# Two transformer blocks in one kernel: another order of work between the output projection and the first weight pairs

## The reference, cut to what matters

```python
x = x + jnp.einsum('bse,ed->bsd', y_mix, w_out[l])
h = rms_norm(x, norm2_g[l])            # x * rsqrt(mean(x*x) + eps) * g
u = causal_dwconv(jnp.einsum('bsd,df->bsf', h, w_up[l]), ffn_conv_w[l])
gate, up = jnp.split(u, 2, axis=-1)
x = x + jnp.einsum('bsf,fd->bsd', jax.nn.gelu(gate) * up, w_down[l])
```

## Time and profile before

| what | value |
|---|---|
| median of 3 runs | 1773.47 us (1772.86 to 1775.33) |
| the profiled execution | 1773.04 us |
| its span in the profile | 1771.3 us |
| mean granted clock of TensorE | 0.982 |
| TensorE busy | 1705.1 us (96%) |
| VectorE busy | 1179.0 us (67%) |
| ScalarE busy | 791.0 us (45%) |
| GpSimd busy | 538.3 us (30%) |

### The profile page before, as it was taken

The page is one execution under the profiler, slowest core; times in us unless marked ns, Lnnn a source line. Parts: engine busy times, 40 slices in busy tenths (PEclk is TensorE's granted clock), DMA queues, the critical chain, the costliest instruction groups (busy, mean ns, idle before and its releaser), DMA issues.

```text
span 1771.3 us, 20806 instructions
## 1 busy us (share of the span) xinstructions
PE 1705.1 (96%) x7516; PEld 1383.2 (78%) x7516; DVE 1179.0 (67%) x1406; ACT 791.0 (45%) x1022; POOL 538.3 (30%) x297
## 2 busy tenths in 40 slices
PE   6999999999859999999999999998999999999998
PEld 5888878888647888888888888887878877666786
DVE  6577671379888776676676789885636455666554
ACT  5566631245434444444444444553422155666531
POOL 4222122100055455455553000003433242444320
PEclk9999999999879999999999999998999999999999
DMA  7111112063302322322323965651322220110251
GB/s 252 48 47 36 47 48 72 24 220 114 119 11 85 95 73 81 95 71 83 91 75 107 342 217 186 224 160 42 119 72 71 84 71 24 36 48 25 89 220 71
DMA packets 159896, 176.96 MB, mean 100 GB/s; under 512 B 13390, under 2 KB 114516, under 8 KB 159828
## 3 DMA queue, kind: packets, MB, share of 16 engines
q1 hardware_dynamic: 157524, 167.67, 29.4%
q10 hardware_dynamic: 2304, 8.39, 1.3%
HBM read 140.38 MB, written 35.65 MB: 99 GB/s over the span
## 4 chain that ended last, share of the span: by engine, by line
PE 87%; DVE 7%; ACT 3%; issue 1%; POOL 1%; DMA 0%; DVEq 0%; ACTq 0%
PE ps L895 27%; PE ps L2282 25%; PE ps L2230 19%; PE ps L2481 5%; PE ps L2451 3%; PE ps L2466 2%; PE ps L2511 2%; PE ps L2454 2%; PE ps L2453 1%; DVE lat L1993 1%; DVE hop_lo_P L1802 1%; PE ps L2438 1%; DVE hop_mix_P L1796 1%; DVE square_dve L1580 0%; DVE scr L1737 0%
## 5 line engine op out<-in xcount | busy, mean ns | idle before, releaser
L919 POOL TENSOR_TENSOR w_lo<-w_raw,w_hi 128x1024 fp32r<-128x1024 f32 x52 | 136.0, 2617 | 622.5 <-ACT w_hi L1035 622.5
L2282 PE MATMUL ps<-hop_hi_P,wop_hi_P 128*128 128x512 f32 x672 | 266.9, 397 | 25.8 <-DVE hop_lo_P L1802 12.8
L2282 PE MATMUL ps<-hop_lo_P,wop_hi_P 128*128 128x512 f32 x672 | 265.8, 395 | 0.0
L2282 PE MATMUL ps<-hop_hi_P,wop_lo_P 128*128 128x512 f32 x672 | 265.3, 395 | 0.0
L895 PE MATMUL ps<-h_hi,w_hi 128*128 128x512 f32 x752 | 235.6, 395 | 13.3 <-DVE h_lo L1565 9.8
L895 PE MATMUL ps<-h_lo,w_hi 128*128 128x512 f32 x752 | 233.7, 392 | 0.0
L895 PE MATMUL ps<-h_hi,w_lo 128*128 128x512 f32 x752 | 233.4, 392 | 0.0
L925 POOL TENSOR_TENSOR wop_lo_P<-pair_raw,wop_hi_P 128x512 fp32r<-128x512 f32 x72 | 113.3, 1574 | 243.6 <-ACT wop_hi_P L1046 243.5
L895 PEld LDWEIGHTS ps<-h_hi,w_hi 128*128 128x128 f32 x752 | 142.0, 190 | 44.9 <-issue 15.9
L2282 PEld LDWEIGHTS ps<-hop_hi_P,wop_hi_P 128*128 128x128 f32 x672 | 128.7, 192 | 55.1 <-issue 13.6
L925 POOL TENSOR_TENSOR wop_lo_P<-pair_sum,wop_hi_P 128x512 fp32r<-128x512 f32 x96 | 132.0, 1376 | 125.4 <-ACT wop_hi_P L1046 125.4
(11 more groups left out here) (337 smaller groups left out, 3274.4 us busy)
## 6 DMA issues: line engine op xcount, KB each, us to landing
pair_raw<-in_w_up SPq DMA_DIRECT2D x48, 512.0 KB, 4.7
w_raw<-in_w_in SPq DMA_DIRECT2D x46, 512.0 KB, 3.9
dn_raw<-gu_park SPq DMA_DIRECT2D x84, 256.0 KB, 3.9
dn_raw<-in_w_down SPq DMA_DIRECT2D x60, 256.0 KB, 3.1
gu_park<-up_cv SPq DMA_DIRECT2D x24, 512.0 KB, 2.6
out_raw<-in_w_out SPq DMA_DIRECT2D x30, 256.0 KB, 3.0
x_tok<-in_x SPq DMA_DIRECT2D x4, 1024.0 KB, 8.0
x_park<-xs SPq DMA_DIRECT2D x1, 4096.0 KB, 14.7
```

Of the source, the lines that this page charges most:

```text
L919: nc.gpsimd.tensor_tensor(lo[:, :], raw[:, :], hi[:, :].bitcast(f32), ALU.subtract).then_inc(w_lo_done, 1)
L2282: mm = nc.tensor.matmul(dst, w[q][:, k, :], x[q][:, k, :], start=a, stop=b, skip_group_check=True)
```

## The change

Five edits, all around the handover:

1. Squares 4 to 11 are taken two per slice in slices 38 to 41 (before: one per slice, 4 to 7, and 8 to 13 after them). ScalarE's square 13 stands behind the first root.
2. The second half's mean squares stand in the middle of P1 of pair 0 (after its first six matmuls), and their spread directly behind P1, ahead of P2.
3. The first eleven weight splits move from GpSimd to VectorE (`first_low`), and so do the two low halves of P3's tokens. GpSimd starts with the twelfth, once those are done.
4. Token sums are made in another order and another way: P5 = B12 - B11, P7 = B22 - B12, P6 = B11 + P7, P4 = B21 - P6. P5's can start after four of the eight second-half tiles. VectorE's list mixes them with weight splits, sums and low parts.
5. TensorE's order of the first two pairs: P1, P2, P1', P2', P5, P6, P5', P7, P6', P4, P3, P7' (' is pair 1; before: P1, P2, P1', P2', P6, P5, P7, P4, P3, P6', P5', P7').

```diff
@@ -376,7 +376,7 @@
         hop_hi_done, hop_sum = sem("hop_hi_done"), sem("hop_sum")
-        hop_lo_pool, hop_lo_dve = sem("hop_lo_pool"), sem("hop_lo_dve")
+        hop_lo_done = sem("hop_lo_done")
         pair_in = [sem(f"pair_in{s}") for s in range(2)]
@@ -479,8 +479,8 @@
                 yield Pair(k // 2, k % 2)
-        FIRST_TURNS = tuple((q, n) for n in (0, 1) for q in ("P1", "P2")) + \
-            tuple((q, 0) for q in ("P6", "P5", "P7", "P4", "P3")) + (("P6", 1), ("P5", 1))
+        FIRST_TURNS = (("P1", 0), ("P2", 0), ("P1", 1), ("P2", 1), ("P5", 0), ("P6", 0), ("P5", 1), ("P7", 0), ("P6", 1),
+                       ("P4", 0), ("P3", 0))
         def nth(q, pair):
@@ -490,16 +490,12 @@
             return place - 1 if isinstance(pair.n, int) and pair.n == PAIRS - 1 and q in ("P4", "P3") else place
-        HOP_HI = ("P1", "P2", "P6", "P5", "P3", "P7", "P4")
-        HOP_SUM = ("P5", "P6", "P4", "P7")
-        HOP_LO_POOL, HOP_LO_DVE = ("P3",), ("P1", "P2", "P6", "P5", "P7", "P4")
+        HOPS = ("P1", "P2", "P5", "P6", "P7", "P3", "P4")
+        HOP_SUM = ("P5", "P7", "P6", "P4")
         def hop_low_wait(eng, q, h):
-            if q in HOP_LO_POOL:
-                eng.wait_ge(hop_lo_pool, 2 * HOP_LO_POOL.index(q) + h + 1)
-            else:
-                eng.wait_ge(hop_lo_dve, 2 * HOP_LO_DVE.index(q) + h + 1)
+            eng.wait_ge(hop_lo_done, 2 * HOPS.index(q) + h + 1)
         def the(pair, n):
@@ -925,13 +921,6 @@
                                         ALU.subtract).then_inc(wop_lo_done, 1)
-            def hop_low(q, h):
-
-                pool.wait_ge(hop_hi_done, 2 * HOP_HI.index(q) + h + 1)
-                k = slice(2 * h, 2 * h + 2)
-                nc.gpsimd.tensor_tensor(hop_lo[q][:, k, :], hop_raw(q, h), hop_hi[q][:, k, :].bitcast(f32),
-                                        ALU.subtract).then_inc(hop_lo_pool, 1)
-
             def odd_lows(i, src):
@@ -948,19 +937,7 @@
                 low(n)
-            for n in (0, 1):
-                for q in ("P1", "P2"):
-                    part_low(q, Pair(0, n))
-            for q in ("P6", "P5"):
-                part_low(q, Pair(0, 0))
-            part_low("P7", Pair(0, 0))
-            for h in range(2):
-                hop_low("P3", h)
-            for q in ("P4", "P3"):
-                part_low(q, Pair(0, 0))
-            for q in ("P6", "P5"):
-                part_low(q, Pair(0, 1))
-
+            pool.wait_ge(wop_lo_done, len(FIRST_TURNS))
             for k in periods(pool):
@@ -1248,11 +1225,11 @@
                 elif 38 <= n:
-                    square(OUT, 4 + n - 38)
+                    for j in (4 + 2 * (n - 38), 5 + 2 * (n - 38)):
+                        square(OUT, j)
             for q in ("P1", "P2"):
                 part_high(q, Pair(0, 0))
-            for j in range(8, 14):
-                square(OUT, j)
+            square(OUT, 12)
             def half_root(h):
@@ -1278,33 +1255,36 @@
                 nc.scalar.copy(s1c[pair.par][:, :], bank(pair, "a")).then_inc(s1c_done, 1)
+            def both_high(q):
+
+                for h in range(2):
+                    hop_high(q, h)
+
             half_root(0)
+            square(OUT, 13)
             square(OUT, 14)
-            for h in range(2):
-                hop_high("P1", h)
+            both_high("P1")
             square(OUT, 15)
             half_root(1)
-            for h in range(2):
-                hop_high("P2", h)
+            both_high("P2")
             part_high("P1", Pair(0, 1))
...
             part_high("P2", Pair(0, 1))
+            for q in ("P5", "P6"):
+                part_high(q, Pair(0, 0))
+            both_high("P5")
             first_sum(Pair(0, 1))
-            for q in ("P6", "P5"):
-                part_high(q, Pair(0, 0))
             act.wait_ge(x1_parked[0], 16)
-            for q in ("P6", "P5"):
-                for h in range(2):
-                    hop_high(q, h)
+            both_high("P6")
+            part_high("P5", Pair(0, 1))
             act.wait_ge(x1_parked[1], 16)
             part_high("P7", Pair(0, 0))
-            for q in ("P3", "P7", "P4"):
-                for h in range(2):
-                    hop_high(q, h)
+            both_high("P7")
+            both_high("P3")
+            part_high("P6", Pair(0, 1))
+            both_high("P4")
             for q in ("P4", "P3"):
                 part_high(q, Pair(0, 0))
-            for q in ("P6", "P5"):
-                part_high(q, Pair(0, 1))
             def ff_first(pair, part):
@@ -1317,8 +1297,7 @@
                                      scale=col(V_FFN + 96 + 24 * part + pair.n)).then_inc(ff_base, 1)
-            for q in ("P4", "P3"):
-                hop_low_wait(act, q, 1)
+            hop_low_wait(act, "P4", 1)
             for k in periods(act):
@@ -1759,8 +1738,9 @@
                 elif 39 <= n:
-                    add_square(OUT, 4 + n - 39)
-            for j in range(7, 12):
+                    for j in (4 + 2 * (n - 39), 5 + 2 * (n - 39)):
+                        add_square(OUT, j)
+            for j in (10, 11):
                 add_square(OUT, j)
@@ -1791,16 +1771,16 @@
                 for h in range(2):
-                    if q != "P5":
-                        dve.wait_ge(hop_sum, (0 if q == "P6" else 2) + h + 1)
+                    if q in ("P6", "P4"):
+                        dve.wait_ge(hop_sum, (2 if q == "P6" else 4) + h + 1)
                     V.tensor_tensor(hop_raw(q, h), x0(h), x1(h), op).then_inc(hop_sum, 1)
-            def hop_low(q):
-                for h in range(2):
-                    dve.wait_ge(hop_hi_done, 2 * HOP_HI.index(q) + h + 1)
+            def hop_low(q, halves=(0, 1)):
+                for h in halves:
+                    dve.wait_ge(hop_hi_done, 2 * HOPS.index(q) + h + 1)
                     k = slice(2 * h, 2 * h + 2)
                     V.tensor_tensor(hop_lo[q][:, k, :], hop_raw(q, h), hop_hi[q][:, k, :].bitcast(f32),
-                                    ALU.subtract).then_inc(hop_lo_dve, 1)
+                                    ALU.subtract).then_inc(hop_lo_done, 1)
             def from_first(pair, out):
@@ -1815,41 +1795,69 @@
                 return token_part(name, h)
-            for p in range(2):
-                last_block(OUT, p)
-                add_square(OUT, 12 + p)
+            def first_low(q, n):
+
+
+                dve.wait_ge(wop_hi_done, nth(q, Pair(0, n)))
+                V.tensor_tensor(wop_lo[q][:, :, :], weight_part(q, Pair(0, n)), wop_hi[q][:, :, :].bitcast(f32),
+                                ALU.subtract).then_inc(wop_lo_done, 1)
+
+            first_low("P1", 0)
+            first_low("P2", 0)
+            last_block(OUT, 0)
+            add_square(OUT, 12)
             half_scale(0)
+            dve.wait_ge(slice_lo, OUT.split(OUT.steps - 1))
+            pair_sums(Pair(0, 0), (0, 1))
+            last_block(OUT, 1)
+            add_square(OUT, 13)
+            pair_sums(Pair(0, 0), (2, 3))
             last_block(OUT, 2)
-            add_square(OUT, 14)
-            dve.wait_ge(slice_lo, OUT.split(OUT.steps - 1))
             dve.wait_ge(rb_done, 2)
...
                 normed(c, T1)
+            add_square(OUT, 14)
+            hop_low("P1", (0,))
             last_block(OUT, 3)
-            normed(4, T1)
+            hop_low("P1", (1,))
             add_square(OUT, 15)
-            hop_low("P1")
-            for c in range(5, KT):
+            for c in range(4, 6):
                 normed(c, T1)
             half_scale(1)
+            for c in range(6, KT):
+                normed(c, T1)
             hop_low("P2")
-            pair_sums(Pair(0, 0), range(4))
             dve.wait_ge(rb_done, 3)
-            for c in range(KT):
+            for c in range(4):
                 normed(c, T2)
+            dve.wait_ge(v_done, 20)
+            hop_add("P5", lambda h: part_of("B12", h), lambda h: part_of("B11", h), ALU.subtract)
+            first_low("P1", 1)
+            for c in range(4, KT):
+                normed(c, T2)
+            hop_low("P5")
+            first_low("P2", 1)
+            first_low("P5", 0)
             dve.wait_ge(v_done, 24)
-            hop_add("P5", lambda h: part_of("B12", h), lambda h: part_of("B11", h), ALU.subtract)
             dve.wait_ge(x1_parked[0], 16)
-            hop_add("P6", lambda h: part_of("B22", h), lambda h: hop_raw("P5", h), ALU.subtract)
+            hop_add("P7", lambda h: part_of("B22", h), lambda h: part_of("B12", h), ALU.subtract)
+            hop_add("P6", lambda h: part_of("B11", h), lambda h: hop_raw("P7", h), ALU.add)
+            pair_sums(Pair(0, 1), (0,))
             hop_add("P4", lambda h: part_of("B21", h), lambda h: hop_raw("P6", h), ALU.subtract)
+            first_low("P6", 0)
             hop_low("P6")
-            hop_low("P5")
-            hop_add("P7", lambda h: part_of("B22", h), lambda h: part_of("B12", h), ALU.subtract)
+            first_low("P5", 1)
             hop_low("P7")
```

(46 more changed lines are left out.)

## The result

The changed kernel takes 1764.15 us (median of 5 runs, 1763.53 to 1765.02), the kernel before 1774.3 in 5 runs: the ratio is 0.9945, with a 95% interval of 0.9931 to 0.996. The forecast was 1763.5, range 1760 to 1769. The profiled execution has a span of 1762.3 us against 1771.3, 9.0 us less.

The account below looks back on a forecast made before the run. VectorE's queue was taken to bound 470 to 534 us, TensorE's products what follows. P4 10.1 us earlier and a new 3.4 us wait put P7's end for pair 1 10.0 us earlier: 1763.5 from the 1773.47 median, range 1760 to 1769.

Parts of the forecast that it names:

- The bound: Handover, 470 to 534 us: VectorE's queue bounds it, TensorE's products what follows; the queue to U3 takes 35.2 us.
- The mean squares inside P1: P1 of pair 0: an earlier spread starts VectorE's second-half normalising at 487.65 instead of 498.33, -10.7 us, the largest term.
- The squares: Before the handover: squares moved up delay the last slice by 1.9 us, but mean squares start 1.0 us earlier.
- The splits on VectorE: VectorE's queue: 11 added weight splits and two token splits cost 8.9 us, paid for by the slow 2.50 us forms vanishing.
- Rival (c): VectorE's handover queue: slow forms belong to these tiles, not GpSimd's doing, so the kernel gets slower, 1793; chance 0.05.
- The new wait: Before P7': TensorE idles 3.4 us for VectorE's sums behind pair 2's load, with 2 us of clock behind it.
- rival (b): Handover: VectorE's queue slower or spread gaining less, the wait before P7' grows, half the queue term left, 1768.5; chance 0.10.
- The clock: TensorE: after each wait of 0.9 us or more the low level returns, charged at 4.4 us, 2.0 us lost.
- Rival (d): 464 to 540 us: seven short waits could keep TensorE at 1.2 GHz, so no gain, 1774.5; chance 0.06.
- The sum: End of P7': 539.8 against 549.8, -10.0 us, with the same work left in both kernels after it.
- (e): P1 of pair 0: square 15's add or the reciprocal comes late, the spread slips behind P2, 1769; chance 0.05.

Follow-up runs that it names:

- order_old: Changed kernel, but TensorE does P5, P6, P7, P4, P3 of pair 0 and only then P5', P6', P7' of pair 1, weight splits likewise; 1769.65 us.
- late_shift: Changed kernel, but the mean squares before the final norm are taken twice, with nothing before 1199 us changed; 1769.28 us.
- changed_again: The changed kernel once more, unaltered, on the chip that ran the next three kernels; 1765.61 us.
- sums_late: Changed kernel, but in pair 0's period VectorE makes the first two sums of pair 2 after the taps instead of ahead of C21; 1766.46 us.
- pool_taps: Changed kernel, but with the first eleven weight splits on GpSimd again and C12 and U2' ahead of the gate taps in pair 0's period; 1767.43 us.

## Why the prediction was right, and where not

**The bound.** VectorE's queue sets the handover: right. Its stretch from the second-half normalising to U3 was put at 35.2 us and took 35.8. The prices of 0.60, 1.15 and 0.68 us held (eleven splits at 0.6 each).

**The mean squares inside P1.** Called the largest term, and it is: 7.0 of 7.6 us go without it. The size was 10.7 at its mark and came out at 9.3 (498.33 to 489.01), or 9.9 counted from S. The eight small matmuls took 1.70 instead of 1.05 at the lower clock, so that root and reciprocal ended at 485.5 instead of 484.1 (0.6 of that is the later S), and the two normalisings and the low parts of P2's tokens that VectorE does next came later. The spread, at 487.5 instead of 485.4, was late too, but it ended at 488.9, before VectorE was free.

**The squares.** +1.9 and -1.0 were expected at their marks; undoing them showed 0.3 us net. Right in kind.

**The splits on VectorE.** This step failed, and moving them back showed it. It said that what pays for 8.9 us of added work is that the slow forms vanish. For the eleven weight splits they gave back 6.2 for 6.6 us, and the later load of pair 2 made it a loss: 1.3 us at P7', 2.3 to 3.0 in H with the clock behind it. The two token splits for P3, the other 2.3 of the 8.9 us, were not tested. Rival (c), that the slow forms are the tiles' own, is refuted: they appear and go with GpSimd's work. The rule that I set beside (c), of the Trainium skill, page "SBUF — State Buffer", section "Who interferes with whom", is borne out on both sides, by 3.46 against 2.36 us for two SBUF operands and by 2.71 unchanged for one in PSUM.

**The new wait.** This term was mis-sized: forecast 3.4 us, measured 5.96. TensorE came to it as forecast, P3 ending at 531.3 for 531.5: P4 started 1.8 us late, but P4 and P3 ran at full clock. VectorE's sum came 2.5 us late. The load took 5.7 us for the 5.9 of the sum, but began at 523.1 instead of 521.1, since the queue ran 1.9 us late, and the two sums of pair 2 took 2.5 us for 1.3, the second of them 1.79 beside GpSimd's split that began at 529.52. What followed, from C21 to U2', took the time forecast. P7' therefore ended 7.1 us earlier (7.7 counted from S), not 10.0. Of rival (b) this much came true: the wait before P7' grew.

**The clock.** The charge of 4.4 us after every wait of 0.9 us or more was too plain: in the changed kernel's trace 2.26, 0.99 and 1.74 us left it high, and in its second trace 2.25 us did not. Rival (d) did not happen; the mean over 464 to 540 us was 0.84, with 1.00 for most of it.

**The sum.** Expected -10.0 in the handover and nothing behind. It was -7.6 there, and the profiled tail gave -2.0 that no step of mine contained. That the forecast of 1763.5 lies 0.65 us from the median is luck: what the handover lacked, the tail gave; the handover alone, with its measured 7.6 us, would have given 1766, still inside the range. (e) did not happen: the spread stood ahead of P2.

**What stays open.** Why the same waits keep or lose the clock from one execution to the next. That the tail's spread is the clock's is shown: TensorE's idle time in it adds up to 14.0 to 14.6 us in all fourteen traces, while the same 3442 matmuls are busy for 772.3 us in both traces of the changed kernel, 774.8 in the kernel before and 776.7 in order_old. T came again in two pairs of traces (794.4 and 794.3, 796.5 twice). In late_shift, 1.95 us of added work went with another outcome behind the same code, but its ten executions lie 6.6 us apart, so one trace does not show that the shift made it. The parts do not add up to the whole either: the experiments account for 7.0 (mean squares) and 1.7 (order), less 2.3 (splits) and 0.3 (squares), 6.1 of the 7.6 us, and the new list of token sums and pair sums was not tested by itself.

## What to carry to other kernels

Look for the instruction whose result the busiest queue waits for, and ask what small piece of another engine's work can be cut in two to let it through: eight tiny matmuls in the middle of one product gave 3.6 us by themselves, and 7.0 of 7.6 once the busiest queue had been cleared for them. Work moved off an engine that blocks its neighbour is free only if it costs less in its new place than the blocking did; here 6.6 us were moved to save 6.2, and a load hung on the last piece. Follow a reordering at least one stage beyond the edited one, since what is covered at the first mark can turn up as a wait at the next.

## What the hardware showed that was not expected

A wait of TensorE of the same length and place kept the full clock in one execution and lost it in another, of one and the same kernel. Before the last slice the changed kernel waits 2.26 us in its first trace and goes on at full clock (the row at 464.73 above: 0.50 us; granted clock 1.00 over 464.7 to 468.3). In its second trace, changed_again, it waits 2.25 us and goes on at the lower level, a granted clock of 0.54 over 465.97 to 469.60:

```profile
465.97 0.79 PE L2238 MATMUL ps<-out_x_hi,out_w_hi 128*128 128x512 f32 x1 [2.25 <-DVE out_x_lo L1658]
466.56 0.63 PE L2238 MATMUL ps<-out_x_lo,out_w_hi 128*128 128x512 f32 x1
```

Ten traces have this wait. Six keep the clock, and in all six TensorE goes on by 464.81 us; four lose it (changed_again, sums_late, pool_taps, late_shift), and in all four it goes on at 465.23 or later. So here the outcome goes with the time at which the wait falls, and not with the kernel. The wait of 2.04 us in the tail does not sort so simply: it is lost at 1430.01, kept at 1430.11 and lost at 1430.51. What decides is not shown.

The length alone does not decide either. The first matmul after the longer wait of 3.90 us before P7' in sums_late took 0.50 us, not 0.79; the lower level came three matmuls later (0.67 over 535.9 to 541.0).

In this kernel such differences add up to 794.3 to 798.4 us for one and the same tail. That is 4 us, more than the 0.2% (3.5 us) at which I held two versions to be distinguishable, so a part of a change should be judged by the stretch it touches, and not by the total alone, and from more than one trace where the stretch holds such waits.
